# Two transformer blocks in fp32: new places and a new order for the 272-column activation tiles

## What is computed

```python
# first block, 256 tokens: attention with a top-64 index, MLP; latent attention, MLP
x = x + dsa_mixer(rms_norm(x, g0), ...);  x = x + squared_relu_mlp(rms_norm(x, g1), w_up, w_down)
x = x + mla_mixer(rms_norm(x, g2), ...);  x = x + squared_relu_mlp(rms_norm(x, g3), w_up, w_down)
x = rms_norm(x, final_norm)

# second block: 16 meta tokens are put in front, so h has 272 rows
h = jnp.concatenate([meta, x], axis=1)
for i in range(2):
    f = swiglu(rmsnorm(h, pre[i, 0]), w1[i, 0], w3[i, 0], w2[i, 0])     # 1024 -> 2816 -> 1024
    h = h + 0.5 * rmsnorm(f, post[i, 0])
    m = causal_multiscale_pool(hn, ...) if i == 0 else diff_attention(hn, w_qkv, w_o, ...)
    h = h + rmsnorm(m, mix_post[i])
    f = swiglu(rmsnorm(h, pre[i, 1]), w1[i, 1], w3[i, 1], w2[i, 1])
    h = h + 0.5 * rmsnorm(f, post[i, 1])
return h[:, 16:]
```

## Time and profile before

| | |
|---|---|
| median of 3 runs | 1713.27 us (1702.89 to 1721.14) |
| profiled execution, its own time | 1697.33 us |
| its span, first to last instruction | 1695.5 us |
| mean granted TensorE clock | 0.995 |
| TensorE busy | 1628.5 us, 96% |
| weight loads busy | 1521.2 us, 90% |
| VectorE, ScalarE busy | 1050.7 and 756.7 us |
| read from main memory | 250.95 MB |

### The profile page before, as it was taken

How to read it: one execution, slowest core, us unless ns; L and a number is a source line. 1 busy time by engine, 2 the same in 40 slices (tenths; PEclk the granted TensorE clock), 3 DMA queues, 4 the chain that set the end, 5 groups by cost and what they waited for, 6 DMA issues and landing times.

```text
span 1695.5 us, 30976 instructions
## 1 busy us (share of the span) xinstructions
PE 1628.5 (96%) x12658; PEld 1521.2 (90%) x12658; DVE 1050.7 (62%) x1261; ACT 756.7 (45%) x1007; POOL 6.4 (0%) x21
## 2 busy tenths in 40 slices
PE   7989999998999999999999999999999999999998
PEld 5858999987899998999987999979999796779997
DVE  7785765568666556666457666466654647576653
ACT  3344554432655434444445444354444336454442
POOL 0000000010000000000000000000000000000000
PEclk9989999999999999999999999999999999999999
DMA  7602566634146675556722556635575351145671
GB/s 168 171 25 73 167 189 192 197 98 110 41 150 198 177 198 167 175 180 188 199 76 76 177 184 195 167 120 173 173 205 167 107 184 58 53 136 187 204 205 59
DMA packets 346818, 252.99 MB, mean 149 GB/s; under 512 B 32590, under 2 KB 345836, under 8 KB 346748
## 3 DMA queue, kind: packets, MB, share of 16 engines
q1 hardware_dynamic: 345136, 250.00, 50.1%
q10 hardware_dynamic: 1612, 2.02, 0.4%
HBM read 250.95 MB, written 1.05 MB: 149 GB/s over the span
## 4 chain that ended last, share of the span: by engine, by line
PE 82%; DVE 12%; ACT 4%; issue 1%; DMA 1%; ACTq 0%; DVEq 0%; SPq 0%
PE acc L473 25%; PE acc L474 25%; PE acc L475 25%; DVE w_low L1330 2%; PE acc L626 2%; PE spare L604 1%; DVE xg_low L1374 1%; ACT w_high L931 1%; PE acc L612 1%; DVE x_state L1526 1%; DVE squares L1359 1%; PE acc L489 1%; DVE evac_a L1524 1%; ACT xg_high L936 1%; PE acc L860 0%
## 5 line engine op out<-in xcount | busy, mean ns | idle before, releaser
L1330 DVE TENSOR_TENSOR w_low<-w_raw,w_high 128x2048 fp32r<-128x2048 f32 (+3 forms) x229 | 540.7, 2361 | 408.2 <-ACT w_high L931 408.0
L473 PE MATMUL acc<-xg_high,w_high 128*128 128x272 f32 (+4 forms) x2592 | 741.0, 286 | 16.5 <-DVE w_low L1330 8.3
L931 ACT ACTIVATE w_high<-w_raw 128x2048 fp32r<-128x2048 f32 (+3 forms) x229 | 451.7, 1973 | 661.4 <-PE acc L475 634.9
L474 PE MATMUL acc<-xg_low,w_high 128*128 128x272 f32 (+4 forms) x2592 | 732.2, 282 | 0.0
L475 PE MATMUL acc<-xg_high,w_low 128*128 128x272 f32 (+4 forms) x2592 | 732.1, 282 | 0.0
L473 PEld LDWEIGHTS acc<-xg_high,w_high 128*128 128x128 f32 (+3 forms) x2592 | 485.0, 187 | 34.2 <-issue 15.7
L474 PEld LDWEIGHTS acc<-xg_low,w_high 128*128 128x128 f32 (+3 forms) x2592 | 484.8, 187 | 3.6 <-issue 3.1
L475 PEld LDWEIGHTS acc<-xg_high,w_low 128*128 128x128 f32 (+3 forms) x2592 | 485.0, 187 | 0.2
L473 PE MATMUL acc<-hidden_high,w_high 128*128 128x256 f32 (+1 forms) x1216 | 343.3, 282 | 2.6 <-DVE w_low L1330 2.5
L475 PE MATMUL acc<-hidden_high,w_low 128*128 128x256 f32 (+1 forms) x1216 | 342.5, 282 | 0.0
L474 PE MATMUL acc<-hidden_low,w_high 128*128 128x256 f32 (+1 forms) x1216 | 342.5, 282 | 0.0
(11 more groups left out here) (198 smaller groups left out, 1061.2 us busy)
## 6 DMA issues: line engine op xcount, KB each, us to landing
w_raw<-in_ffn_w_dram SPq DMA_DIRECT2D x88, 1024.0 KB, 5.4
w_raw<-in_ffn_w_dram SPq DMA_DIRECT2D x32, 1408.0 KB, 7.0
w_raw<-in_mlp_w_up_dram SPq DMA_DIRECT2D x32, 1024.0 KB, 5.4
w_raw<-in_mlp_w_down_dram SPq DMA_DIRECT2D x32, 1024.0 KB, 5.5
w_raw<-in_attn_w_qkv_dram SPq DMA_DIRECT2D x12, 1024.0 KB, 5.1
w_raw<-in_a_w_in_dram SPq DMA_DIRECT2D x18, 256.0 KB, 4.4
w_raw<-in_a_w_in_dram SPq DMA_DIRECT2D x4, 1024.0 KB, 8.0
w_raw<-in_a_w_out_dram SPq DMA_DIRECT2D x4, 1024.0 KB, 5.0
```

The source lines that it names most:

```text
L473: pe.matmul(dst, high_w, high, start=first, stop=False)
L474: pe.matmul(dst, high_w, low, start=False, stop=False)
L931: act.activation(whi[c % 2][:, 0:SIZES[c]], raw[c % 2][:, 0:SIZES[c]], ACT.Copy).then_inc(S["w_high"], 1)
L1330: dve.tensor_tensor(wlo[c % 2][:, s], raw[c % 2][:, s], whi[c % 2][:, s].bitcast(F32), ALU.subtract)\
```

## The change

With 272 columns, rows of XH, XL, HH and HL are 1088 bytes apart instead of 1280, and the low rows begin STEP = 16 elements (64 bytes) into their tensors, so that row k's high part begins at 64(k + 1) modulo 256 and its low part at 64(k + 2). The 256-column layers keep their rows. A unit of `wide` with 272 columns that has no `ready` waits runs over all rows for the first half of the output channels, then for the second. The freed bytes let the window table lie in one piece behind the hidden rows, loaded by one DMA.

```diff
-ROW = (4 * T2 + LINE - 1) // LINE * LINE // 4
-def row(T):
-    return ROW if T == T2 else T
+STEP = 16
+ROW = (4 * SEQ + LINE - 1) // LINE * LINE // 4 + LINE // 4
+def low_row(h, T):
+    return h + STEP if T == T2 else h
...
+        def layer_rows(t, tiles, skip):
+            return {SEQ: t[:].rearrange("p (k t) -> p k t", t=ROW),
+                    T2: t[:, skip:skip + tiles * T2].rearrange("p (k t) -> p k t", t=T2)}
...
-        XH = place("xg_high", [P, KD, ROW], F32R)
-        XL = place("xg_low", [P, KD, ROW], F32R)
+        XH, XL = (layer_rows(place(name, [P, KD * ROW], F32R), KD, skip)
+                  for name, skip in (("xg_high", 0), ("xg_low", STEP)))
...
-        band = [place(f"pool_band{i}", [P, 2 * BAND], offset=t + 4 * KF2 * ROW)
-                for i, t in enumerate((region, region + 4 * KF * SEQ))]
+        band = place("pool_band", [P, len(WINDOWS) * BAND], offset=region + 4 * KF2 * T2)
```

In `wide`, the units of "up" and of the projections:

```diff
-                for k in range(KD):
-                    if ready is not None and ready[k] is not None:
+                order = [(k, m) for k in range(KD) for m in range(2)] if T == SEQ or ready is not None else \
+                    [(k, m) for m in range(2) for k in range(KD)]
+                for k, m in order:
+                    if m == 0 and ready is not None and ready[k] is not None:
                         pe.wait_ge(*ready[k])
-                    for m in range(2):
...
-                        ins = three(acc[u % 2][0:rows_, m, 0:T], *w, XH[:, k, 0:T], XL[:, k, 0:T],
-                                    k == 0, k == KD - 1)
+                    ins = three(acc[u % 2][0:rows_, m, 0:T], *w, XH[T][:, k, 0:T], XL[T][:, k, 0:T],
+                                k == 0, k == KD - 1)
```

In `down`:

```diff
-                            h = (q * kc + k) * row(T)
+                            h = (q * kc + k) * T
-                                        HL[:, h:h + T], q == 0 and k == 0, q == chunks - 1 and k == kc - 1)
+                                        HL[:, low_row(h, T):low_row(h, T) + T], q == 0 and k == 0, q == chunks - 1 and k == kc - 1)
```

In VectorE's writer of `hidden_low` (ScalarE's writer of `hidden_high` likewise, without the shift), and the window table's load:

```diff
-                    h, r = j * row(T), row(T)
-                    where = slice(h, h + 2 * r) if it is None else ds(it * 2 * r + h, 2 * r)
-                    two = lambda v: v.rearrange("p (k t) -> p k t", k=2)[:, :, 0:T]
-                    dve.tensor_tensor(two(HL[:, where]), a, two(HH[:, where]).bitcast(F32), ALU.subtract)\
+                    h = j * T
+                    where = lambda h: slice(h, h + 2 * T) if it is None else ds(it * 2 * T + h, 2 * T)
+                    two = lambda v: v.rearrange("p (k t) -> p k t", k=2)
+                    dve.tensor_tensor(two(HL[:, where(low_row(h, T))]), a, two(HH[:, where(h)]).bitcast(F32), ALU.subtract)\
...
-            for i in range(2):
-                act.dma_start(band[i][:], window[:, i * 2 * BAND:(i + 1) * 2 * BAND]).then_inc(S["window_in"], 16)
+            act.dma_start(band[:], window).then_inc(S["window_in"], 16)
```

More of the change, by code:

```diff
@@ L308, in two_blocks_kernel @@
         Z = alias("pool_mixed", [P, 3, D])
-        band = [place(f"pool_band{i}", [P, 2 * BAND], offset=t + 4 * KF2 * ROW)
-                for i, t in enumerate((region, region + 4 * KF * SEQ))]
-        assert KF2 * ROW + 2 * BAND <= KF * SEQ
+        band = place("pool_band", [P, len(WINDOWS) * BAND], offset=region + 4 * KF2 * T2)
+        assert 4 * (KF2 * T2 + len(WINDOWS) * BAND) <= 4 * KF * SEQ
         sub[0] = region
@@ L495, in wide @@
                 wait_unit(g, j, it, per)
-                for k in range(KD):
-                    if ready is not None and ready[k] is not None:
+                order = [(k, m) for k in range(KD) for m in range(2)] if T == SEQ or ready is not None else \
+                    [(k, m) for m in range(2) for k in range(KD)]
+                for k, m in order:
+                    if m == 0 and ready is not None and ready[k] is not None:
                         pe.wait_ge(*ready[k])
-                    for m in range(2):
[L500 to L503, removed]
-                        ins = three(acc[u % 2][0:rows_, m, 0:T], *w, XH[:, k, 0:T], XL[:, k, 0:T],
-                                    k == 0, k == KD - 1)
+                    if tiles is None:
+                        w, rows_ = cols(c, k * 256 + m * P, k * 256 + (m + 1) * P), P
+                    else:
+                        w, rows_ = tiles(c, k, m)
+                    ins = three(acc[u % 2][0:rows_, m, 0:T], *w, XH[T][:, k, 0:T], XL[T][:, k, 0:T],
+                                k == 0, k == KD - 1)
                 ins.then_inc(S["w_used"], 1)
@@ L760, in latent_unit @@
                     for k in range(KK):
-                        ins = three(dst, *weights(k), XH[:, k0 + k, 0:SEQ], XL[:, k0 + k, 0:SEQ],
+                        ins = three(dst, *weights(k), XH[SEQ][:, k0 + k, 0:SEQ], XL[SEQ][:, k0 + k, 0:SEQ],
                                     k == 0, k == KK - 1)
@@ L839, in _ @@
                         t = slice(t0, t0 + nt)
-                        pe.matmul(dst, XH[:, k, t], hw, start=k == 2 * q, stop=False)
-                        pe.matmul(dst, XH[:, k, t], lw, start=False, stop=False)
-                        ins = pe.matmul(dst, XL[:, k, t], hw, start=False, stop=k == 2 * q + 1)
+                        pe.matmul(dst, XH[T2][:, k, t], hw, start=k == 2 * q, stop=False)
+                        pe.matmul(dst, XH[T2][:, k, t], lw, start=False, stop=False)
+                        ins = pe.matmul(dst, XL[T2][:, k, t], hw, start=False, stop=k == 2 * q + 1)
                 if q % 2:
@@ L849, in _ @@
             keep_busy(sp[1][:, 1], 3)
-            pe.wait_ge(S["window_in"], 32)
+            pe.wait_ge(S["window_in"], 16)
             for j, bank in enumerate((acc[0], sp[0], acc[1], acc[0])):
@@ L857, in _ @@
                 for m in range(2):
-                    o, ch = j % 2 * BAND, j * 256 + m * P
+                    o, ch = j * BAND, j * 256 + m * P
                     for i, (t0, nt) in enumerate(TOKENS):
-                        ins = pe.matmul(bank[:, m, t0:T2], Z[0:nt, i, ch:ch + P], band[j // 2][0:nt, o:o + T2 - t0],
+                        ins = pe.matmul(bank[:, m, t0:T2], Z[0:nt, i, ch:ch + P], band[0:nt, o:o + T2 - t0],
                                         start=i == 0, stop=i == 2)
@@ L935, in high_parts @@
                 for k in range(a, b):
-                    ins = act.activation(XH[:, k, 0:T], src[:, k, T0:T0 + T], ACT.Identity,
+                    ins = act.activation(XH[T][:, k, 0:T], src[:, k, T0:T0 + T], ACT.Identity,
                                          scale=gain[:, gcol + k:gcol + k + 1])
@@ L1021, in unit @@
                     if gcol is not None:
-                        dst = XH[:, j, 0:SEQ] if it is None else XH[:, ds(it * 2 + j, 1), 0:SEQ]
+                        dst = XH[SEQ][:, j, 0:SEQ] if it is None else XH[SEQ][:, ds(it * 2 + j, 1), 0:SEQ]
                         src = X[:, j, META:] if it is None else X[:, ds(it * 2 + j, 1), META:]
@@ L1064, in pair @@
                     act.wait_ge(S["dve_evac"], at(g.r0 + j + 2, it, 2))
-                    h, r = j * row(T), row(T)
-                    dst = HH[:, h:h + 2 * r] if it is None else HH[:, ds(it * 2 * r + h, 2 * r)]
-                    act.activation(dst.rearrange("p (k t) -> p k t", k=2)[:, :, 0:T], tb[1][:, :, 0:T], ACT.Copy)\
+                    h = j * T
+                    dst = HH[:, h:h + 2 * T] if it is None else HH[:, ds(it * 2 * T + h, 2 * T)]
+                    act.activation(dst.rearrange("p (k t) -> p k t", k=2), tb[1][:, :, 0:T], ACT.Copy)\
                         .then_inc(S["hid_high"], 1)
@@ L1141, in out_high @@
                         act.wait_ge(S["o_turned"], n.add("o_turned"))
-                        dst = XH[:, 4 * half_:4 * half_ + 4, i * P:(i + 1) * P]
+                        dst = XH[SEQ][:, 4 * half_:4 * half_ + 4, i * P:(i + 1) * P]
                         src = sp[i][:, half_, :].rearrange("p (k t) -> p k t", k=4)
@@ L1373, in low_parts @@
                     gc = gcol + k
-                    ins = dve.scalar_tensor_tensor(XL[:, k, 0:T], src[:, k, T0:T0 + T], gain[:, gc:gc + 1],
-                                                   XH[:, k, 0:T].bitcast(F32), ALU.mult, ALU.subtract)
+                    ins = dve.scalar_tensor_tensor(XL[T][:, k, 0:T], src[:, k, T0:T0 + T], gain[:, gc:gc + 1],
+                                                   XH[T][:, k, 0:T].bitcast(F32), ALU.mult, ALU.subtract)
                 ins.then_inc(S["xg_ready"], 1)
@@ L1492, in down_unit @@
                     tile = lambda v: v[:, at_, META:]
-                    part = lambda v: v[:, at_, 0:SEQ]
+                    part = lambda v: v[SEQ][:, at_, 0:SEQ]
                     dve.tensor_tensor(tile(X), tile(X), acc[(g.u0 + j) % 2][:, 0:1, 0:SEQ], ALU.add)\
@@ L1642, in out_low @@
                         if gcol is None:
-                            ins = dve.tensor_tensor(XL[dst], src, XH[dst].bitcast(F32), ALU.subtract)
```

(3 more changed lines are left out.)

## The result

The changed kernel took 1729.46 us, the median of 18 runs (1710.38 to 1735.69), against 1718.76 us for the kernel before in 18 runs (1702.89 to 1726.26): ratio 1.0079, 95% interval 1.0046 to 1.0112. So it is slower by 0.5 to 1.1%: at its middle under the 1% that the prediction set for "no change", but not nothing.

A forecast was written before the change was run, and what follows sets the result against it. TensorE was taken to bound the kernel, its filled 272-column stages lasting matmul count times a 123.3 ns step. Four terms of 0 summed to no change, 1713.3 us; likeliest case 1697 to 1730, 8-in-10 range 1666 to 1738.

The forecast's parts named there:

- The frame: 272-column stages: TensorE is never fed late, so time is matmul count times step; 5328 matmuls, one nanosecond is 5.3 us.
- the forecast class: Whole kernel: no effect of places, cancelling effects, or a gain or loss under 3.2 ns per 272-column matmul; chance 0.44.
- Step 1: Places of the 272-column moving rows: the new offsets change the matmul step by 0 ns.
- the c_k rows: Attention key rows, 1088 bytes apart, plain fp32: score groups took 0.73 us at all four places, taken as zero effect.
- The bounds: Limits on the effect of places per 272-column matmul: gain at most 10.0 ns, loss at most 4.3 ns.
- The second support: First projection's third unit: weight tiles move in 32-byte steps past fixed rows, yet line 474 keeps the fast pace, 275/276/283 ns.
- The slower rival: Every 272-column unit: the fixed place keeps the better pace, varying places lose it; 4.3 ns each, +22.9 us, 1736; chance 0.22.
- The faster rival: 272-column matmuls: stepping 64 bytes forward mends a place collision; 120.0 ns, -17.6 us, up to -53 us, middle 1678; chance 0.34.
- Step 2: Order in ordinary 272-column up and qkv units, all rows per half of the output channels: costs and gains nothing.
- Step 3: Window table in one DMA, issued at about 663 us, landing bounded by 11.4 us, covered by 226 us: taken as 0.
- Step 4: ScalarE and VectorE write hidden pairs contiguously instead of with a 48-element gap: 0 either way.
- The marks named ahead: Line 474's median duration at 272 columns: 286 to 287 no effect, 283 or 276 to 277 faster, over 290 slower; plus starts.

The follow-up runs named there:

- the bench: Kernels leaving the whole reference out, TensorE alone streaming fp32r matmuls at varied places: 272 columns stepped at 123.4 ns with rows at 64, 125.0 with the changed kernel's places.
- The last bench: TensorE alone, reference left out, with shorter weight loads, one weight tile reloaded, or plain fp32: plain fp32 229.2 ns at every place, reloaded tile 123.3 to 126.7 ns.

## Why the prediction was right or wrong

The forecast was no change, at 1713, with 44% for within 1%; measured was +0.8%, inside the range and inside that class. The frame held: TensorE's stages are filled, each nanosecond of step is 5.3 us, and 1.75 ns gave 9.3 us, beside 6 to 9 between the heaps' medians and 10.7 between the medians of all runs. That the forecast class came out is partly luck. It rests on an effect of nothing, and there is an effect; 1.75 ns is small enough for the class of under 3.2 ns, where the bench has places that cost up to 3.4 ns.

Step 1 failed, by which places cost nothing. I took 0 ns from the c_k rows and named their weakness, that they are plain fp32. The last bench shows that this is enough to explain them: plain fp32 shows no place at 229.2 ns, fp32r with full loads shows it by up to 3.4 ns. The nearest row by pitch and column count was far by kind of matmul, which is what mattered. The bounds (10.0 ns gain, 4.3 ns loss) held.

The second support, failed likewise: 256 columns, and only eleven of line 474's matmuls in one of two paces. In the bench, 256 columns with the low weights elsewhere stepped at 118.2, against 113.3 with all weights in one place in the same run, so the weights' place does count there too. What kept that short unit at its fast pace was not tried.

The slower rival had the mechanism right, that the fixed place of before is a good pace which the walk gives up, and its price too high: 4.3 ns, borrowed from the two paces of the 256s, where the walk costs 1.75. "No pace can settle" was wrong as well: the walk settles at 125.0 in every pass, a steady pattern.

The faster rival asked that the step forward mend the end of a tile. The steps of the changed kernel, averaged over 714 to 800 us, repeat every 12 matmuls, the length of four rows: those to a place 64 further average 124.5 ns (single ones 121.0 to 127.3), those back 126.0 (122.7 to 128.2). On the mean neither comes to the 123.3 of standing still at 64. Whether the forward move is the better one stays open: every step back is also the one behind a low row.

Step 2, no effect of the order: shown, for tiles all in one place; with the walk it saves 0.5 ns, about 2 us. Step 3: the window table landed 6.8 us after one issue at 686.9 us, long before it is read. Step 4: VectorE and ScalarE are busy for 1051.2 and 757.3 us, before 1050.7 and 756.7.

The marks named ahead served: the median duration went to 287 and 288, between "no effect" and "slower", and the starts gave the size. What was not foreseen is how far two profiles can lie apart for reasons outside the change: 18 us for the clock in the first attention, and 6 for the pace of the 256s. The prediction put the spread of the timed runs, 18 us, down to the pace of the 256s alone; at its own 4.3 us for 1000 matmuls that would take some 4200 of them, and the two heaps point to the clock instead.

## What to carry to other kernels

In streams of fp32r matmuls with a full weight load each, try the byte offset of the moving rows against that of the weights in a bare stream first, with the column count and the order of the real kernel, and in several passes; for 272 columns the bench gave this kernel's steps to 0.1 ns. Take the nearest row by kind of matmul, not by shape. Compare two profiles by the step inside filled stretches, and set apart clock and pace before giving a difference to the change.

## What the runs showed of the hardware

fp32r streams with a load each pay for their length too: from the bench, 111.7 ns at 144 columns, 120.0 at 264, 133.4 at 288, 146.7 at 320 and about 233 at 512, where plain fp32 takes 229.2 for each record of 272 columns, 114.6 for each pass if a record is two passes (a reading that no row shows). 320 and 512 columns at 2.4 GHz would be 133.3 and 213.3 ns (estimates), so the surcharge is 13 and 20 ns. At 272 columns, the only count at which shorter loads were tried, it does not leave with them: the trace has a load at 94 ns with 16 weight columns and at 188 with 128, and the step is 124.4 ns or more at 16. The reported duration follows the step: it was 160 to 165 ns longer at each of these counts, so that it tells the pace, but is not what a matmul costs. Why, and why one float of offset moves the step by 3 to 6 ns, stays open: that load and stream meet in SBUF is argued from the last bench, not shown, and which reads collide was not resolved. The Trainium skill ("TensorE: Matmul & The Clock Gate", Part 2, step 1) has a weight load take no bandwidth from the running matmul; at 128 weight columns the measured steps, 123.3 to 126.7 ns by offset alone, do not agree with that.
